# A top-k step of a gather stage on VectorE, computed one group later

## The reference

```
def peer(h, wq, keys1, keys2, u_tab, v_tab):      # chunks of 128 tokens
    q = (xc @ wq).reshape(128, 8 heads, 2, 128)
    s1 = einsum('chd,hnd->chn', q[:, :, 0], keys1)   # 128 keys a head
    s2 = einsum('chd,hnd->chn', q[:, :, 1], keys2)
    v1, i1 = top_k(s1, 16);  v2, i2 = top_k(s2, 16)
    cand = v1[..., :, None] + v2[..., None, :]       # 256 a head
    cidx = i1[..., :, None] * 128 + i2[..., None, :]
    best, pos = top_k(cand, 16)
    eidx = take_along_axis(cidx, pos)                # 16 experts a head
    g = softmax(best)
    a = einsum('chkd,cd->chk', u_tab[eidx], xc)      # one row of 1024 an expert
    return einsum('chk,chkd->cd', gelu(a) * g, v_tab[eidx])
```

## Time and profile before

| | |
|---|---|
| median of 3 runs | 1824.59 us (1818.69 to 1826.14) |
| the profiled execution | 1826.14 us, span 1824.2 us |
| PE, DVE, ACT, POOL busy | 82%, 49%, 17%, 28% of the span |
| DMA queue 0 (POOL's gathers) | 268.84 MB |
| gathers, first and last start | 1044.4 us, 1806.9 us |

### The profile page before, as it was taken

One profiled execution on the slowest core, in us unless ns is written; L12 is line 12 of the kernel. 1 busy time (PEld: TensorE's weight loads), 2 busy tenths in 40 slices (PEclk: granted clock), 3 DMA queues, 4 the chain that ended last, 5 costly groups with the idle time before them and its releaser, 6 DMA issues.

```text
span 1824.2 us, 17400 instructions
## 1 busy us (share of the span) xinstructions
PE 1502.5 (82%) x6106; PEld 831.6 (46%) x6106; DVE 885.5 (49%) x1991; ACT 311.3 (17%) x634; POOL 501.9 (28%) x540
## 2 busy tenths in 40 slices
PE   7999999999999999898999973285757585858576
PEld 6867564434434343484687773132323232323222
DVE  3986143323232222366401573867575747471754
ACT  3113222101111110203300203021111111120010
POOL 2000000000000000000000055567575757676765
PEclk9999979999999999999999986587878787878789
DMA  9639466999999999641124287799999989999997
GB/s 329 227 141 385 167 258 290 425 430 428 430 428 429 429 428 426 235 167 46 34 95 149 98 293 298 284 355 393 341 393 342 392 334 386 343 395 356 385 355 279
DMA packets 135272, 565.35 MB, mean 310 GB/s; under 512 B 11497, under 2 KB 17430, under 8 KB 122732
## 3 DMA queue, kind: packets, MB, share of 16 engines
q1 hardware_dynamic: 60588, 295.66, 40.6%
q0 software_dynamic: 74416, 268.84, 38.8%
q10 hardware_dynamic: 208, 0.09, 0.0%
HBM read 563.49 MB, written 1.06 MB: 309 GB/s over the span
## 4 chain that ended last, share of the span: by engine, by line
PE 71%; issue 9%; POOL 8%; DMA 6%; DVE 4%; ACT 1%; another core or an unknown queue 1%; SPq 0%; POOLq 0%; DVEq 0%; ACTq 0%
PE psum L405 50%; PE psum L999 19%; POOL ring L1150 8%; DMA ring<-in_peer_v_dram,attnT 2%; DMA ring<-in_ada_w_dram 2%; DVE scratch L2093 1%; DMA arena<-in_hf_w_dram 1%; DMA ring<-in_peer_u_dram,attnT 1%; PE psum L413 0%; PE psum L785 0%; PE psum L791 0%; SPq L1013 0%; PE psum L860 0%; DVE ring L1961 0%
## 5 line engine op out<-in xcount | busy, mean ns | idle before, releaser
L999 PE MATMUL psum<-ring,arena 128*128 128x512 f32 x904 | 443.6, 645 | 244.1 <-DMA ring<-in_peer_v_dram,attnT 158.7
L1150 POOL DMA_INDIRECT ring<-in_peer_u_dram,attnT x251 | 236.9, 944 | 1173.6 <-DVE attnT L2067 1030.0
L999 PEld LDWEIGHTS psum<-ring,arena 128*128 128x128 f32 x904 | 183.5, 206 | 503.6 <-issue 370.7
L405 PE MATMUL psum<-ring,arena 128*64 128x512 f32 (+1 forms) x1552 | 343.8, 594 | 1.4 <-DVE arena L1822 1.4
L2093 DVE CUSTOM_DVE_ANT_0 scratch<-ring,psum 128x1024 f32<-128x1024 f32 x251 | 301.2, 1220 | 89.2 <-DMA ring<-in_peer_u_dram,attnT 70.9
L405 PE MATMUL psum<-actT,ring 128*128 128x256 f32 (+1 forms) x1424 | 270.6, 351 | 29.4 <-issue 27.9
L1150 POOL DMA_INDIRECT ring<-in_peer_v_dram,attnT x256 | 246.7, 964 | 129.9 <-issue 81.9
L405 PEld LDWEIGHTS psum<-actT,ring 128*128 128x128 f32 x1424 | 240.8, 199 | 58.2 <-issue 35.2
L405 PEld LDWEIGHTS psum<-ring,arena 128*64 128x64 f32 (+1 forms) x1552 | 110.5, 137 | 219.3 <-issue 205.8
L1453 ACT ACTIVATE arena<-ident,attnT 128x128 f32<-128x128 f32 x226 | 80.3, 395 | 361.2 <-issue 135.7
L1864 DVE TENSOR_TENSOR arena<-arena,psum 128x512 f32<-128x512 f32 x16 | 16.9, 1058 | 203.9 <-PE psum L405 203.9
(11 more groups left out here) (380 smaller groups left out, 1198.7 us busy)
## 6 DMA issues: line engine op xcount, KB each, us to landing
ring<-in_w_gate_dram SPq DMA_DIRECT2D x32, 2048.0 KB, 11.9
ring<-in_w_up_dram SPq DMA_DIRECT2D x32, 2048.0 KB, 16.3
ring<-in_w_down_dram SPq DMA_DIRECT2D x32, 2048.0 KB, 14.1
ring<-in_w_in_dram SPq DMA_DIRECT2D x15, 2048.0 KB, 14.4
ring<-in_ada_w_dram SPq DMA_DIRECT2D x12, 2048.0 KB, 11.4
ring<-in_w_out_dram SPq DMA_DIRECT2D x4, 2048.0 KB, 8.7
ring<-in_peer_wq_dram SPq DMA_DIRECT2D x4, 2048.0 KB, 10.5
ring<-in_w_attn_out_dram SPq DMA_DIRECT2D x2, 2048.0 KB, 8.8
```

Of the source, the lines that this page charges most:

```text
L405: return nc.tensor.matmul(o, lhsT, rhs, start=(k == 0), stop=(k == n - 1))
L999: last = nc.tensor.matmul(psum[:, 4 + 2 * t + n, :], diag[:, i, :], row_buf(b, use)[:, n * 512:(n + 1) * 512], start=first, stop=final)
L1150: pool.indirect_dma_start(out=row_buf(b, use), out_offset=None, in_=tab, in_offset=bass.IndirectOffsetOnAxis(ap=rowid[:, j // 4, k:k + 1], ...
```

## The change

DVE's program had computed the picks two groups ahead of the dots; now it computes them one group ahead. The other engines' programs are the same.

```diff
@@ -2148,7 +2148,6 @@
             picks_of(1)
             dots_of(0)
             weigh(0)
-            picks_of(2)
             for j in range(1, LAST + 1):
                 dots_of(j)
                 if j == 5:
@@ -2156,8 +2155,8 @@
                 if j == 7:
                     final_norm(0)
                 weigh(j)
-                if j + 2 <= LAST:
-                    picks_of(j + 2)
+                if j < LAST:
+                    picks_of(j + 1)
             add_rows(LAST - 1)
             add_rows(LAST)
             into_residual(1)
```

## The result

| | before | after |
|---|---|---|
| median | 1822.24 us (4 runs, 1818.69 to 1826.14) | 1844.03 us (4 runs, 1839.21 to 1849.79) |
| ratio | | 1.012, interval 1.0083 to 1.0158 |
| the profiled execution | 1826.14 us, span 1824.2 | 1844.83 us, span 1842.8 |

The change makes the kernel slower by 1.2%. I had forecast 1827 us and no change; the rival on the slower side came true in part: it had put 1852 us. The two profiled executions differ by 18.7 us, their spans by 18.6, about as the medians do (21.8), so the spans can be taken apart.

The account below looks back on a forecast made before the run. The gather stage was taken as a ring of POOL, PE and DVE with no engine full. A start gain of 9.0 us and 11.2 us more in five stretches gave +2.2, so 1827 us as a median, range 1809 to 1844.

Parts of the forecast that it names:

- the rival on the slower side: POOL's stops in the six u turns are its own and stay, 4.2 us each: 1852 us; chance 0.29 with partial forms.
- Its stops within the u turn: POOL's waits inside a later u turn, 4.2 us, put down to PE, were to go, leaving 39.8 us a turn.
- S + 78.0: S is the start of a v turn; PE was to have added up the v rows 78.0 us later.
- the check: Last u gather put down to PE, number 23, starts at S + 82.6, after PE's end, so it would not wait.
- The start: First v and u2 turns of the gather stage: POOL's 15.28 us wait falls to 0.30, gaining 9.0 us (4.2 to 15.0).
- From S to the end of the picks: In each later stretch the u turn waits for picks ending 54.0 us after the v turn's start; stretch 93.8 us.
- The last term: The stage's end, from 1714.50 us on in the profile before: old order, 109.5 us remain, no change.
- ACT's wait: ACT's gate_exp(j + 1), queued ahead of the 32 diagonals, waits for the picks just computed; counted as 0.
- The slow stretch: Part of a v turn where gaps between instructions stretch the picks; forecast to stay at the same distance from S.
- the faster rival: The slow stretch shrinks or falls elsewhere, picks take under 39 us, u turns never wait: 1810 us; chance 0.25.

Follow-up runs that it names:

- half_sums: The changed kernel with PE adding up only the first 512 of the 1024 columns of every v row: 1869.86 us, ratio 1.0266.
- two_behind: The kernel before with the change's new start, picks(2) and picks(3) both behind weigh(1), then two groups ahead again: 1821.0 us, ratio 1.0004.
- exp_behind: The changed kernel with ACT's gate_exp(j + 1) moved behind diagonals(j): 1841.73 us, ratio 1.0118.
- four_before: The kernel before, with POOL limited to at most four gathers under way: 1900.4 us, ratio 1.0471.
- short_picks: The changed kernel with the picks of groups 2 to 7 replaced by a copy of earlier row numbers: 1804.65 us, ratio 0.9943.
- five_before: The kernel before with at most five gathers under way: 1766.68 us (1.0226) on the fast chip, 1825.81 us (1.0029) on a slower one.
- six_before: The kernel before with at most six gathers under way: 1736.21 us (1.0044) on the fast chip, 1822.82 us (1.0006) on a slower one.

## Why the prediction was wrong, step by step

The forecast sum was +2.2 us and the spans show +18.6; 16.4 us have to be found.

- **The step that failed: "Its stops within the u turn (4.2 us) should go, because they come from PE."** A u turn was to take 39.8 us. The five of the stretches took 42.6, 43.1, 43.2, 42.9 and 43.1 us: 3.2 too much on the mean, 16.0 in all; turn u2 took 43.7, 3.9 too much. That is 19.9 us, more than the whole miss. (Before, the five took 44.1 us on the mean, so 1.1 of the 4.2 did go.) In half_sums these stops go, so they do come from PE's work. What fell was the conclusion: that a turn which starts later finds PE done. I had put the v rows' end at S + 78.0 and it is at S + 77.4, but the check compared gather 23 with the end of PE's record, as if POOL could go on at that moment. At 1325.57 POOL got the event of row 23 some ten us after the record had its sum done. The rows of before held the warning: the gather of 1328.36 needs the sum of row 24, 28 matmuls before the end of PE's last run, which at the run's mean (34.42 us for 75) was 13 us before 1334.7, at about 1322. POOL went on some 6 us later than that. Why the events come late stays open.
- **The start, -9.0 forecast, -3.7 measured.** The wait of 15.28 us is gone and the first v turn begins at 1148.83, 3.3 us ahead of my 1152.1. Turn u2 begins at 1209.21, 1.3 us behind my 1207.9. The rest is the stop in u2. Two_behind has the same start and measures as before.
- **From S to the end of the picks, 54.0 forecast.** Measured until the first u gather: 51.1, 54.0, 52.9, 53.8 and 53.1, mean 53.0: right, and 1.0 a stretch better, 5.0 in all. The last term is +0.2. Together: 3.9 + 16.0 + 1.3 - 5.0 + 0.2 = 16.4 us.
- **ACT's wait, 0 forecast.** Right: exp_behind takes it away and gains nothing that can be measured.
- **The slow stretch doesn't move away or shrink.** Right, and so the faster rival fell: picks(3) take 43.3 us from nearly the same distance to S. The Trainium skill says in Runtime: NRT & Kernel Launch, section Instruction fetch mechanics, that crossing a block of instructions is mostly hidden. Four_before agrees: the same instructions at the same place in DVE's program take 14.5 to 15.0 us, so it isn't the place in the code alone that stretches them. That loading is slowed by the gathers themselves no run separates, but the DMA view speaks against it: from 1256 to 1304 before has four packets of the queues of kind instruction and four_before three, too few for a gap at nearly every instruction.
- **The slower rival.** It said that the stops stay when the turn starts later, at 4.2 us each. They stay, at 3.2 on the mean and 3.9 in u2, against its 4.2; its reason, that they are POOL's own, is not borne out, since they go in half_sums. I had given it 0.29, because of one stop labelled PE whose condition I could work out. The label was right; the calculated end was not when POOL could go on.

The time, 1844.03 us, came out at the very top of the range, which ended at 1844.

Shown, then: the loss lies in u turns that wait for picks which take 45 us in place of 15 (short_picks leaves them out, and the loss is gone), and whose own stops stay. It isn't transfer volume, the start or ACT. **Open** is what slows all engines' small instructions. It needs more than four gathers under way (four_before has none of it, five_before some, six_before nearly all of it on a chip of the slower kind), it ends a few us after the gathers under way have landed, half the bytes don't change it, and one chip of five doesn't have it with up to six under way; at 1728.81 us it can hardly have it without a limit, but neither before nor after was profiled there. Events that arrive late would fit the gaps and POOL's stops alike, but can't be all: PE's record of before has five single matmuls from 1287.66 to 1298.86 with 1.1 to 2.8 us idle ahead of each, and a v row has four, within which the program waits for nothing.

## What to carry to other kernels

Before moving a producer from "early" to "just in time", read its duration in the place where it will stand, not at its best: these picks are 15 us of work that took 43 to 46. And don't take a stop as absorbed because the turn around it starts later: compare the stops in the trace you have with the record of the work that they wait for. If they end well after it, that record doesn't tell when a later turn can go on. A gain at a stage's start of one wait (15 us here) is worth only what the next wait leaves of it (3.7 us in the trace, nothing measurable in two_behind).

## What the runs showed of the hardware that I had not expected

- With POOL issuing gathers of 128 rows each 1.245 us, DVE's, ACT's and PE's instructions came with gaps for up to 35 us in a v turn, and the picks beside them took 41 to 46 us; with at most four gathers under way, 14.5 to 15.0.
- Halving a gather's bytes (367 to 184 GB/s) changed the time by 0.1%.
- ACT and POOL, waiting for the same sum of PE, went on within 0.3 us of each other (1325.33 and 1325.57), some ten us after PE's record had it done; in turn u2, for the sum of row 30, at 1240.28 and 1240.51, 14 us after the record's end.
- The same kernel took 1728.81 us on one chip and 1816.57 to 1822.22 on four others, 5% more, so kernels can be compared only on the same chip.
- Halving PE's sums made after slower still (1869.86 us, against 1841.73 and 1843.67 of its like on that chip): with no stop of POOL in the v turn its gathers ran on, and DVE's slow stretch lasted until they had landed.
